# Hand-over between the two MLP stages: when the right-hand tiles of the third and fourth pair are split, where three additions stand, and where one weight load stands in the queue

## The reference, cut to what matters

```python
def sq_relu_mlp(h, w1, w2):
    return jnp.square(jax.nn.relu(h @ w1)) @ w2      # w1: 1024 x 4096, w2: 4096 x 1024
...
        h = modulate(rmsnorm(x, norm_mlp_g[i]), sh2, sc2)
        x = x + g2[:, None, :] * sq_relu_mlp(h, mlp_w1[i], mlp_w2[i])
```

## Time and profile before

| | |
|---|---|
| time, median of 3 runs | 2476.96 us (2475.19 to 2477.6) |
| profiled execution, its time | 2473.96 us |
| its span, first to last instruction | 2472.0 us |
| mean granted TensorE clock | 0.985 |
| TensorE busy | 2393.0 us, 97% of the span |
| VectorE busy | 1712.7 us, 69% |
| ScalarE busy | 1117.1 us, 45% |
| GpSimd busy | 521.4 us, 21% |

### The profile page before, as it was taken

How to read it: one execution, slowest core, us unless ns; L and a number is a source line. 1 busy time by engine, 2 the same in 40 slices (tenths; PEclk the granted TensorE clock), 3 DMA queues, 4 the chain that set the end, 5 groups by cost and what they waited for, 6 DMA issues and landing times.

```text
span 2472.0 us, 32746 instructions
## 1 busy us (share of the span) xinstructions
PE 2393.0 (97%) x11248; PEld 1943.4 (79%) x11248; DVE 1712.7 (69%) x2690; ACT 1117.1 (45%) x1946; POOL 521.4 (21%) x453
## 2 busy tenths in 40 slices
PE   7999999999999999999999899999999999999998
PEld 2577888788878888888788788888788897886677
DVE  7788777888787554277766787785642227998873
ACT  2355444544434223145454544342431227887851
POOL 0210001433233000200000342320110003557731
PEclk9899999999999999999999999998999999999999
DMA  8715665754436631325553753540453472336521
GB/s 312 272 57 206 222 223 191 264 178 159 133 106 182 215 107 51 123 98 179 194 172 125 255 201 122 161 130 18 162 145 128 146 187 72 92 98 171 156 69 68
DMA packets 272392, 380.13 MB, mean 154 GB/s; under 512 B 63600, under 2 KB 173296, under 8 KB 272240
## 3 DMA queue, kind: packets, MB, share of 16 engines
q1 hardware_dynamic: 272240, 378.17, 47.2%
HBM read 277.44 MB, written 106.69 MB: 155 GB/s over the span
## 4 chain that ended last, share of the span: by engine, by line
PE 86%; DVE 6%; issue 3%; POOL 2%; ACT 1%; DMA 1%; SPq 0%; DVEq 0%; POOLq 0%; ACTq 0%
PE banks L2721 22%; PE banks L2723 22%; PE banks L2722 22%; PE banks L3290 2%; PE banks L3308 2%; PE banks L2814 2%; PE banks L3075 1%; PE banks L3076 1%; PE banks L3077 1%; PE banks L3277 1%; PE banks L2762 1%; PE banks L3278 1%; PE banks L2876 1%; POOL probs L1456 1%; DMA stage<-hidden 1%
## 5 line engine op out<-in xcount | busy, mean ns | idle before, releaser
L2721 PE MATMUL banks<-Hhi,Whi 128*128 128x512 f32 x1760 | 700.0, 398 | 33.3 <-DVE X L2397 14.5
L2723 PE MATMUL banks<-Hhi,Wlo 128*128 128x512 f32 x1760 | 691.0, 393 | 0.0
L2722 PE MATMUL banks<-Hlo,Whi 128*128 128x512 f32 x1760 | 690.9, 393 | 0.0
L2721 PEld LDWEIGHTS banks<-Hhi,Whi 128*128 128x128 f32 x1760 | 334.3, 190 | 112.5 <-issue 32.2
L2722 PEld LDWEIGHTS banks<-Hlo,Whi 128*128 128x128 f32 x1760 | 334.6, 190 | 70.7 <-issue 2.4
L2723 PEld LDWEIGHTS banks<-Hhi,Wlo 128*128 128x128 f32 x1760 | 333.8, 190 | 70.8
L2721 PE MATMUL banks<-T,Whi 128*128 128x512 f32 x720 | 282.1, 392 | 0.0
L2723 PE MATMUL banks<-T,Wlo 128*128 128x512 f32 x720 | 281.4, 391 | 0.0
L2722 PE MATMUL banks<-T,Whi 128*128 128x512 f32 x720 | 281.2, 391 | 0.0
L1658 ACT ACTIVATE Whi<-stage 128x512 fp32r<-128x512 f32 (+2 forms) x180 | 105.0, 583 | 225.9 <-PE banks L2723 225.9
L2397 DVE SCALAR_TENSOR_TENSOR X<-banks,mod,X 128x512 f32<-128x512 f32 x180 | 134.0, 745 | 92.1 <-PE banks L2723 91.4
(11 more groups left out here) (259 smaller groups left out, 4102.1 us busy)
## 6 DMA issues: line engine op xcount, KB each, us to landing
stage<-w SPq DMA_DIRECT2D x58, 1024.0 KB, 6.7
stage<-hidden SPq DMA_DIRECT2D x224, 256.0 KB, 3.7
hidden<-slot SPq DMA_DIRECT2D x196, 256.0 KB, 2.1
stage<-ada_w SPq DMA_DIRECT2D x48, 1024.0 KB, 6.1
x_saved<-X SPq DMA_DIRECT2D x32, 512.0 KB, 3.9
stage<-w_in SPq DMA_DIRECT2D x13, 1024.0 KB, 6.2
X<-x_saved SPq DMA_DIRECT2D x24, 512.0 KB, 5.2
stage<-sgu_in SPq DMA_DIRECT2D x8, 1024.0 KB, 6.7
```

Of the source, the lines that this page charges most:

```text
L2721: nc.tensor.matmul(out_bank, whi, xhi, start=start, stop=False, skip_group_check=onto)
L2722: nc.tensor.matmul(out_bank, whi, xlo, start=False, stop=False, skip_group_check=onto)
L2723: return nc.tensor.matmul(out_bank, wlo, xhi, start=False, stop=stop, skip_group_check=onto)
```

## The change

Three edits. First, a table `LATE` gives the steps at which the tiles of pairs 2 and 3 are split. Before, (2,0) to (2,6) were split at steps 2, 3, 4, 5, 6, 7, 7 of pass 0 and (3,0) to (3,6) at steps 0 to 6 of pass 1. Now (2,0), (2,1), (2,2) come at steps 5, 6, 7 of pass 0, (2,3) to (2,6) at steps 0 to 3 of pass 1, (3,0) and (3,1) at steps 6 and 7 of pass 1, and (3,2) to (3,6) at steps 0 to 4 of pass 2. `LOADS` follows: loads 25 to 28 move from pass 0 to pass 1, loads 31 to 35 from pass 1 to pass 2. Second, in the last unit VectorE does the first addition before it splits side 1 and tile (0,1), and the second and third addition before side 2 and tiles (0,2), (1,0). Third, SyncE issues the weights of pass 1 after the first four right-hand tiles and no longer before them.

```diff
@@ -153,13 +153,21 @@
+LATE = {2: ((0, 5), (0, 6), (0, 7), (1, 0), (1, 1), (1, 2), (1, 3)),
+        3: ((1, 6), (1, 7), (2, 0), (2, 1), (2, 2), (2, 3), (2, 4))}
+
+
 def right_steps(t):
 
-    pairs = [p for p in range(CHUNKS) if made_during(p) == t]
+    pairs = [p for p in range(CHUNKS) if made_during(p) == t and p not in LATE]
     steps = [[] for _ in range(len(SIDES) + 1)]
     for n, p in enumerate(pairs):
         for q in range(len(SIDES)):
-            steps[min(q + 2 * n + (2 if t == 0 else 0), len(SIDES))].append((p, q))
+            steps[min(q + 2 * n, len(SIDES))].append((p, q))
+    for p in LATE:
+        for q, (late, step) in enumerate(LATE[p]):
+            if late == t:
+                steps[step].append((p, q))
     return steps
@@ -1096,8 +1104,10 @@
                 if last:
                     load_pass(T, l, 0)
+                    for n in range(4):
+                        load_raw(T, l, n)
                     load_pass(T, l, 1)
-                    for n in range(RAW):
+                    for n in range(4, RAW):
                         load_raw(T, l, n)
@@ -2349,15 +2359,21 @@
-                after(1)
+                if not last:
+                    after(1)
                 dve.wait_ge(first_copied, g + 1)
                 join(g, 0, U2[:], 2, "B", U1[:])
+                if last:
+                    after(1)
...
-                after(2)
+                if not last:
+                    after(2)
                 dve.wait_ge(joined, 5 * g + 1)
                 join(g, 1, U1[:], 3, "C", U2[:])
+                if last:
+                    after(2)
                 dve.wait_ge(joined, 5 * g + 2)
                 join(g, 2, m_full["22"][:], 0, "D", U1[:])
```

## The result

| | before | changed kernel |
|---|---|---|
| median | 2475.56 us (8 runs) | 2482.29 us (7 runs) |
| profiled execution: time, span | 2473.96, 2472.0 | 2481.32, 2479.4 |
| mean granted TensorE clock | 0.985 | 0.985 |

The ratio is 1.0030 with a 95% interval of 1.0020 to 1.0039: the change makes the kernel slower by 5.0 to 9.7 us, with 7.4 in the middle. The forecast was 2482.4 us, 5.4 more than the 2476.96 us that the kernel before had when the prediction was made. An eighth run of the changed kernel, at a granted clock of 0.555, took 4018.79 us and is left out of the median and the ratio.

The account below looks back on a forecast made before the run. TensorE was busy for 97% of the span, so only its gaps could be won. Layer 0 +1.6, layer 1 -0.3, clock +3.3 and pass 2 +0.8 gave +5.4 on 2476.96: 2482.4 us, range 2472.5 to 2487.

Parts of the forecast that it names:

- Edit 2: Last unit, layer 1: additions first remove 3.6 us of stall and 1.7 of slow matmuls; new 3.1 stall in pass 0.
- Edit 1 in pass 0: Pass 0, layer 0: with (2,0) out of C1's way, product 5 starts at 452.35 instead of 454.26, 1.9 us won.
- Start of pass 1: First product of pass 1 waits for (2,0): 1.7 us sooner in layer 0, 3.7 in layer 1.
- Start of pass 2: Product 0 waits for (3,0): 19.3 us after pass 1, stall some 3.6; layer 0 loses 1.6, layer 1 wins 0.3.
- two engines that only share the rate of their ports: VectorE beside GpSimd in pass 1: rate sharing instead of an exclusive lock would put pass 2's start about 1 us lower.
- The clock: After the stall at pass 2's start, matmuls run slowly for a while: 1.65 us in each layer, +3.3 together.
- the first rival: The clock stays up at pass 2: only +2.1 us, 2479.1; chance 0.18, shared with all gains and waits cancelling.
- Pass 2: Within pass 2, one blocked tile in every second case, late by 0.7: 0.4 us per layer, bounds 0 and 3.
- Edit 3 at nothing: Last unit: first four tiles land some 2 us earlier, but VectorE's subtraction ends where it did; priced at nothing.
- Sum: Both hand-overs: layer 0 +1.6, layer 1 -0.3, clock +3.3, pass 2 +0.8, giving +5.4 us.

Follow-up runs that it names:

- experiment 1: Kernel before plus additions first and pass 1 weights issued after the first four right-hand tiles, split steps as before; ratio to before 0.9991.
- experiment 5: Kernel before with only VectorE's additions in the last unit moved first; ratio to before 0.9994.
- experiment 2: Kernel before with only the later split steps of pairs 2 and 3 (`LATE`) and their loads; ratio to before 1.0021.
- experiment 3: Changed kernel with the seven tiles of pair 3 split two steps sooner; ratio to before 0.9991.
- experiment 7: Changed kernel with the seven tiles of pair 3 split three steps sooner; ratio to before 0.9989.
- experiment 4: Changed kernel with GpSimd computing only 16 of 512 columns in each of four hidden sums of pass 1; ratio to before 0.9990.
- experiment 6: Kernel before with only the pass 1 weights issued after the first four right-hand tiles; ratio to before 1.0000.

## Why the prediction was right, step by step

- **Edit 2.** Forecast: product 5 of layer 1's unit starts without a stall, 3.6 and 1.7 us removed; a new stall of 3.1 before product 4 of pass 0. Measured: no stall, unit 24.37 to 19.47, new stall 3.10. That this is one mechanism, work put off in a full queue, experiments 1 and 5 show: of the 4.9 and 3.7 us that the unit wins, pass 0 leaves 0.4 and 0.6, part of it by the clock.
- **Edit 1 in pass 0.** Forecast 1.9 won by keeping (2,0) out of C1's way. In experiment 2, which has nothing else, product 5 starts 1.9 sooner after the start of pass 0 in both layers, and the pass is 1.8 and 1.9 shorter.
- **Start of pass 1.** Forecast 1.7 and 3.7 sooner; measured 1.47 and 3.23.
- **Start of pass 2.** Forecast 19.3 us after pass 1, a stall of 3.6; measured 19.44 and 19.43, stalls of 3.38 and 3.35. Experiments 3 and 7 move it with the steps of pair 3 alone, and experiment 4 with GpSimd alone. It did not come out about 1 us lower, as the prediction had put it for two engines that only share the rate of their ports.
- **The clock.** This term was too large. Forecast: both stalls cost 1.65; only layer 1's did, 1.6 (pass 2 took 21.40 there and 19.82 in layer 0). So the first rival, the clock that stays up, held in layer 0. In layer 1 pass 0 ran at 0.80 too, after the 3.10 stall, which I had not charged; from product 5 to pass 1 it took 4.85 where I had 4.55. The Trainium skill, "TensorE: Matmul & The Clock Gate", section "What's actually happening", has a free-running check of activity. The trace agrees: here 3.38 cost nothing, and in experiment 4 one stall of 2.09 cost 1.6 and its twin nothing.
- **Pass 2.** Forecast +0.4 each, by tiles blocked once in every second case; measured +0.78 in layer 0 and, without the clock, the same in layer 1. One tile is late in each layer, (3,5). It stands behind a weight side whose subtraction takes 1.57 us beside a GpSimd operation (489.18 to 490.48), and TensorE restarts 0.1 after the tile, some 0.4 us late; the rest are delays of 0.1 and less. VectorE and TensorE, after, layer 0:

```profile
489.46 1.57 DVE L2329 TENSOR_TENSOR Wlo<-stage,Whi 128x512 fp32r<-128x512 f32 x1
490.95 0.68 DVE L2337 TENSOR_TENSOR Hlo<-stage,Hhi 128x512 fp32r<-128x512 f32 x1
491.73 0.47 PE L2737 MATMUL banks<-Hhi,Whi 128*128 128x512 f32 x1 [0.26 <-issue]
```

- **Edit 3 at nothing.** The sum was nearly right, the reason wrong: the earlier tiles did shorten a unit, by 1.2 us beside edit 2 and by 0.5 alone, and pass 0 took most of it back.
- **Sum.** Layer 0 +2.8 (forecast 3.7), layer 1 +2.7 (1.8), together 5.4 as forecast. That it fits to the tenth is luck: the clock that stayed up took 1.65 off, and two starts of pass 1 that were 0.2 and 0.5 too hopeful, two of pass 2 by 0.1 and two long passes 2 by 0.4 each put it back. Whole runs say 7.4 with an interval from 5.0 to 9.7, which holds it. Why the middle lies 2 us above the hand-over's growth stays open: the profiled spans differ by as much in stretches with the same instructions, and I had no experiment on that.

## What to carry to other kernels

When a consumer waits behind a full in-order queue, moving one item later pays only if the next deadline in that queue can bear it: list the deadlines of all that is pushed back before moving. An item placed at "after product n" that product n+1 needs costs the whole latency through the engines, whatever the queues hold: 2.3 to 2.4 us in experiment 4. And count what stands beside the queue: here GpSimd work that looked off the path set the pace of VectorE, and a load that was covered by 3 us became the bound as soon as its user moved forward.

## What the runs showed that I had not expected

The clock's fall can't be told from the length of a stall between 2 and 3.5 us. The start of pass 2 is one place of the program, reached here each time after a pass 1 at a clock of 1.00, and these are its stalls:

| kernel, layer | stall, us | clock in pass 2 | pass 2, us |
|---|---|---|---|
| changed, 0 | 3.38 | 1.00 | 19.82 |
| changed, 1 | 3.35 | 0.92 | 21.40 |
| experiment 2, 0 | 3.38 | 0.92 | 21.43 |
| experiment 2, 1 | 3.36 | 1.00 | 19.80 |
| experiment 4, 0 | 2.09 | 0.92 | 21.39 |
| experiment 4, 1 | 2.09 | 1.00 | 19.82 |
| experiment 3, both | 1.08 | 1.00 | 19.14, 19.16 |

A change that leaves stalls of 2 us or more here has its time scattered by 1.6 us for each of them, and one traced execution can credit or charge these 1.6 us to the wrong edit, as in experiment 6.
